# The inverse roots of 14 norms taken on two columns per token and spread by products with the identity; the output written in four transfers

## The chip, the cores and the metric

One NeuronCore of a Trainium2 chip runs the whole program. Its engines work side by side and wait for each other on semaphores: TensorE (PE: matmuls, and PEld: the loads of their stationary operand), VectorE (DVE), ScalarE (ACT), GpSimd (POOL) and SyncE (SP, which here issues the transfers of the weights and of the output). The metric is the device time of one execution in microseconds; a time is the median of several runs.

## What is computed

The reference runs two stacks of transformer-like blocks over 256 tokens with 1024 features (`x`), the first beside a second sequence of 256 context tokens (`ctx`). Each block opens its two halves with an RMS norm whose result is scaled and shifted by vectors made from a condition:

```python
def rms_norm(x, g):
    xf = x.astype(jnp.float32)
    y = xf * lax.rsqrt(jnp.mean(xf * xf, axis=-1, keepdims=True) + RMS_EPS)
    return (y * g.astype(jnp.float32)).astype(x.dtype)

def modulate(h, shift, scale):
    return h * (1 + scale) + shift
...
h = modulate(rms_norm(x, norm_g[i, 0]), sh1, sc1)
```

In the first stack the output of a mixer or of an MLP is normed as well before it is added to `x`. The second stack adds it without a norm, and ends in `rms_norm_2(x, final_g)`, which is the output. All told the kernel takes 17 such norms: one at the start, and 16 for which the line numbers below stand. What matters of them is one number for each token, the inverse root of the mean square over its 1024 features.

## The kernel before

Activations lie features first: a tile is [128 features, 256 tokens], and `KT` = 8 tiles make the 1024 features of a sequence. The sequences are called segments, `CTX` = 0 and `X` = 1. A sum over features is therefore a sum over partitions, and TensorE makes it: `sums_tensor` (L867) multiplies a 128x128 matrix of ones with the squares of tile k and adds the eight tiles up in PSUM. Since all 128 columns of the ones give the same sum, the result stands in every one of the 128 rows, and the root (`root_scalar`, L904, on ACT) and the reciprocal (`inverse_root_vector`, L911, on DVE) are taken on the whole [128, 256] tile `RS`. A float32 product is two records in the trace, so the eight products of one segment are 16 records. For six of the norms POOL adds the first six squares up beforehand, and TensorE has three products (6 records) instead of eight.

The places have names by what is normed: `y_x01`, `y_x02`, `y_x11`, `y_x12` are outputs of a mixer or an MLP, `n2_0`, `n1_1`, `n2_1`, `n1_2`, `n2_2`, `n1_3`, `n2_3` the residual stream, `final` the output. `y_x01`, `n2_0`, `y_x02` and `n1_1` exist for both segments.

At a place of the residual stream the order is: `x_squares_scalar` (ACT, L935) squares a tile, the sums follow tile by tile (L883), then the root (L907), the reciprocal (L914), `scaled_vector` (DVE, L943: one instruction per tile), then `high_scalar` (ACT, L974), which rounds the shifted tile, and `low_vector` (DVE, L988), which keeps what rounding left. The products that follow (`MLP0.columns` and others, L549) multiply high by the weights' high part, high by their low part, and low by high, eight tiles each, so a tile of output is 24 products. Where y is normed, `normed_residual_vector` (L993) multiplies pairs of tiles of y by the inverse root (L1003, four instructions) and adds them to x (L1008, eight instructions); the order on DVE is pair 0, pair 1, add 0, 1, pair 2, add 2, 3, pair 3, add 4 to 7. So a place of y is followed at once by a place of x: `y_x01` by `n2_0`, `y_x02` by `n1_1`, `y_x11` by `n2_1`, `y_x12` by `n1_2`. These are called pairs below.

Every engine works its instructions off in the order in which the program gives them. The blocks at the end of the program (L3818 to L4066) write that order out by hand, one list for each engine. Around `n2_0` DVE's list is: reciprocal and residual for X, the same for CTX, then for X and after it for CTX: reciprocal, `scaled_vector`, `low_vector`. `unread_products(pe, n, bank)` (L890) puts n float32 products of 512 columns into TensorE's list whose result nobody reads.

PSUM has eight banks. `take_bank` (L445) gives them out by a counter, and TensorE waits until the holder before has been marked "taken":

```python
b = pool[bank_state["next"] % len(pool)]
bank_state["next"] += 1
if bank_state["holder"][b] is not None:
    pe.wait_ge(*after("taken", *bank_state["holder"][b]))
```

The pool is banks 0 to 6 where nothing else is said; the sums have bank 6 for X and bank 5 for CTX, and a call with one fixed bank moves the counter too. In the kernel before, 112 calls precede the first tile of `mlp0_tensor`, 488 the first of `mlp_split_tensor` and 708 the first of `od_tensor`. `mlp0_tensor` (L1597) takes the banks of its first four tiles before its first product, then works out those four tiles for X, and after them for CTX. The weights go through a ring of four slots that SP fills when TensorE or DVE has released a block.

## Time and profile before

| | |
|---|---|
| time, median of 3 runs | 2351.47 us (2351.32 to 2355.02) |
| the profiled execution | 2352.81 us, its span 2350.9 us |
| mean granted clock of TensorE | 0.973 |
| busy in the span | PE 95%, PEld 79%, DVE 61%, ACT 41%, POOL 4% |
| reciprocals of the 16 norms (L914) | 16 of 1.75 us on DVE |
| unread products, sums, roots | L894, L883, L907 |
| transfer of the output | 1024 KB, 3.9 us from issue to landing |

Busy time says that an engine had work, not that the end depended on it. A PE that is busy counts loads and the drain of its pipeline too, and may stream few columns. The granted clock is a share of full speed: 1.00 is 2.4 GHz, 0.50 is 1.2 GHz. In a timeline a line is `start, duration, engine, source line, operation`, consecutive records of one kind are merged, and the brackets say how long the engine sat idle before it and who ended that.

### The profile page before, as it was taken

What the parts mean: (1) busy time and instruction counts of PE and PEld (TensorE: products, weight loads), DVE (VectorE), ACT (ScalarE), POOL (GpSimd) and SP (SyncE); (2) the same over time, 40 slices, a digit from 0 to 9 for tenths busy, and PEclk for the clock granted to TensorE, in tenths of its full rate; (3) what the DMA queues carried; (4) which work ended last, traced back from release to release, by engine and by line L of the source; (5) the groups of instructions that cost most, each with busy time, mean ns of one, the idle gap of its engine ahead of it and who ended that gap; (6) DMA issues with size and microseconds to landing.
All of it is one profiled execution on the core that took longest, in us unless ns stands there. A gap on an engine that the chain in (4) does not pass through costs nothing.

```text
span 2350.9 us, 48675 instructions
## 1 busy us (share of the span) xinstructions
PE 2242.8 (95%) x21596; PEld 1852.2 (79%) x21596; DVE 1427.9 (61%) x2467; ACT 971.5 (41%) x1716; POOL 85.4 (4%) x83
## 2 busy tenths in 40 slices
PE   8999999999999999999999999998999999899997
PEld 5864478888867789999998899895677879677786
DVE  3273536867657366887763653465475876656576
ACT  2244333332313223433322563344355655545565
POOL 1000000000010000000000001020000002000000
PEclk9999999999999989999999999998999999999999
DMA  8335237656522100000003446444355853204484
GB/s 355 108 111 213 89 128 302 252 214 233 215 99 104 40 1 4 4 4 4 13 4 129 142 176 239 197 180 179 126 219 210 337 218 126 72 1 179 177 339 181
DMA packets 47314, 348.13 MB, mean 148 GB/s; under 512 B 5264, under 2 KB 5280, under 8 KB 5760
## 3 DMA queue, kind: packets, MB, share of 16 engines
q1 hardware_dynamic: 45936, 334.52, 37.8%
q0 software_dynamic: 1168, 10.50, 1.1%
q8 instruction: 170, 2.79, 0.5%
q14 instruction: 40, 0.33, 0.0%
HBM read 343.95 MB, written 1.05 MB: 147 GB/s over the span
## 4 chain that ended last, share of the span: by engine, by line
PE 52%; DVE 8%; ACT 3%; issue 1%; DVEq 0%; ACTq 0%
PE banks L549 10%; PE banks L2245 6%; PE banks L2257 5%; PE banks L1037 4%; PE banks L3179 3%; PE banks L3180 3%; PE banks L3181 3%; PE banks L3210 2%; PE banks L3212 2%; PE banks L3211 2%; PE banks L2097 1%; PE banks L2304 1%; PE banks L561 1%; PE banks L2279 1%; PE banks L3228 1%
## 5 line engine op out<-in xcount | busy, mean ns | idle before, releaser
L527 DVE TENSOR_TENSOR mlp_w_low<-weight_slots,mlp_w_high 128x2048 fp32r<-128x2048 f32 x64 | 146.5, 2289 | 186.8 <-ACT mlp_w_high L518 186.8
L527 DVE TENSOR_TENSOR moe_w_low<-weight_slots,moe_w_high 128x2048 fp32r<-128x2048 f32 x96 | 217.9, 2289 | 61.6 <-ACT moe_w_high L518 60.8
L518 ACT ACTIVATE mlp_w_high<-weight_slots 128x2048 fp32r<-128x2048 f32 x64 | 122.4, 1912 | 177.8 <-PE banks L549 122.6
L518 ACT ACTIVATE moe_w_high<-weight_slots 128x2048 fp32r<-128x2048 f32 x96 | 181.7, 1914 | 23.6 <-PE banks L3212 19.8
L1037 PE MATMUL banks<-arena,weight_slots 128*128 128x256 f32 (+1 forms) x512 | 140.7, 436 | 3.0 <-DVE arena L2846 1.5
L3179 PE MATMUL banks<-moe_w_high,slots_x 128*128 128x512 f32 x320 | 130.6, 408 | 2.8 <-DVE moe_w_low L527 2.8
L1037 PEld LDWEIGHTS banks<-arena,weight_slots 128*128 128x128 f32 x512 | 97.8, 192 | 43.7 <-issue 33.6
L3180 PE MATMUL banks<-moe_w_low,slots_x 128*128 128x512 f32 x320 | 127.6, 399 | 0.0
L3181 PE MATMUL banks<-moe_w_high,slots_x 128*128 128x512 f32 x320 | 127.5, 398 | 0.0
L686 DVE SCALAR_TENSOR_TENSOR arena<-weight_slots,silu_c,arena 128x256 f32<-128x256 f32 x240 | 99.4, 483 | 0.0
L2245 PE MATMUL banks<-arena 64*64 64x64 f32 (+1 forms) x1600 | 81.9, 234 | 0.0
L2245 PEld LDWEIGHTS banks<-arena 64*64 64x64 f32 x1600 | 78.3, 139 | 0.5 <-issue 0.3
L1281 ACT ACTIVATE arena<-arena 128x256 f32<-128x256 f32 (+2 forms) x128 | 62.3, 489 | 38.8 <-DVE arena L1225 38.7
L864 POOL TENSOR_TENSOR arena<-arena 128x256 f32<-128x256 f32 (+1 forms) x30 | 36.5, 1216 | 1031.9 <-ACT arena L1683 407.8
L3179 PEld LDWEIGHTS banks<-moe_w_high,slots_x 128*128 128x128 f32 x320 | 60.7, 190 | 15.8 <-DVE moe_w_low L527 3.2
L3181 PEld LDWEIGHTS banks<-moe_w_high,slots_x 128*128 128x128 f32 x320 | 60.7, 190 | 14.7
L549 PE MATMUL banks<-quarter_high,mlp_w_high 128*128 128x512 f32 x256 | 67.4, 400 | 3.5 <-ACT quarter_high L1674 3.4
L3180 PEld LDWEIGHTS banks<-moe_w_low,slots_x 128*128 128x128 f32 x320 | 60.9, 190 | 12.4
L614 PE MATMUL banks<-weight_slots,arena 128*32 128x256 f32 x896 | 65.1, 414 | 4.5 <-DMA weight_slots<-weights 4.5
L549 PE MATMUL banks<-both_high,mlp_w_high 128*128 128x512 f32 (+1 forms) x288 | 68.3, 375 | 0.9 <-ACT both_high L974 0.8
L2257 PE MATMUL banks<-weight_slots 64*64 64x32 f32 x2048 | 66.6, 221 | 1.2 <-DVE weight_slots L2719 1.2
L2504 ACT ACTIVATE weight_slots<-banks 128x256 f32<-128x256 f32 x64 | 23.0, 382 | 107.7 <-DVE weight_slots L2709 107.2
(454 smaller groups left out, 5211.1 us busy)
## 6 DMA issues: line engine op xcount, KB each, us to landing
weight_slots<-weights SPq DMA_DIRECT2D x318, 1024.0 KB, 4.9
arena<-small POOLq DMA_DIRECT2D x1, 2560.0 KB, 9.0
arena<-x_t POOLq DMA_DIRECT2D x1, 2048.0 KB, 12.8
arena<-bias POOLq DMA_DIRECT2D x1, 2048.0 KB, 11.4
constants<-consts POOLq DMA_DIRECT2D x1, 1395.0 KB, 17.9
out_t<-arena SPq DMA_DIRECT2D x1, 1024.0 KB, 3.9
parameters<-params POOLq DMA_DIRECT2D x1, 763.0 KB, 21.8
arena<-pool_inv POOLq DMA_DIRECT2D x1, 512.0 KB, 14.6
```

Source lines behind the costliest of these rows:

```text
L518: nc.scalar.activation(self.pair(j)[0], slot(j, 0, SLOT), ACT.Copy).then_inc(*act.step("high", j))
L527: nc.vector.tensor_tensor(self.pair(j)[1], slot(j, 0, SLOT), self.pair(j)[0], ALU.subtract).then_inc(*v.step("used", j))
L549: ins = nc.tensor.matmul(out, self.pair(j)[part][:, at:at + P], x(k), start=start and n == 0 and k == 0, stop=stop and n == 2 and k == til ...
L614: ins = nc.tensor.matmul(psum(7, n % 2 * 256, 256, slice(32 * g, 32 * g + 32)), Z[:, 22 + 32 * k - n // 2 * 2:][:, 0:32], slot(j, k, 256), ...
L686: nc.vector.scalar_tensor_tensor(a_, w, c, a_, ALU.mult, ALU.add).then_inc(*v.step())
L1037: ins = nc.tensor.matmul(psum(b, 0, w), slot(j, k, 256, i * P, P), moving(k), start=(k == 0), stop=(k == KT - 1))
L1281: nc.scalar.activation(S[:, u % N, c:c + w], S[:, u % N, c:c + w], ACT.Exp, bias=M[:, u % N, 3 + j:4 + j], accum_out=M[:, u % N, 6 + j:7 + ...
L2245: ins = nc.tensor.matmul(psum(b, n * width, width, r), lhs, rhs, start=(i == 0), stop=(i == len(ts) - 1))
L2257: ins = nc.tensor.matmul(psum(b, p * 32, 32, half(h)), lhs(p, half(h)), rhs(p, half(h)), start=opens, stop=True, skip_group_check=True)
L3179: nc.tensor.matmul(psum(b), x_hi, wh, start=(k == 0), stop=False)
L3180: nc.tensor.matmul(psum(b), x_hi, wl, start=False, stop=False)
L3181: ins = nc.tensor.matmul(psum(b), x_lo, wh, start=False, stop=(k == KT - 1))
```

## The change

- At 14 places (all but `y_x02` and `n1_1` for CTX) the sums are turned around: the squares are the stationary operand, 128 tokens at a time, and one column of ones moves. The sums then stand one token to a row, in two columns. Root and reciprocal work on [128, 2].
- `spread_root_tensor` brings them back to [128, 256]: two products of a column of `RS`, broadcast to 128x128, with the identity. The result stands in the upper half of the bank of the sums, and `scaled_vector`, `normed_residual_vector` and `final_vector` read it there. The bank is "taken" only when the last of them that needs it has run: the eighth instruction of L943, or the fourth of L1003.
- TensorE's list: the unread products that stood before and after the sums are split, two ahead of each spread at most places, the rest behind; none ahead of the spreads of `n2_0`, where both segments' sums come first, then both spreads, then `mlp0_tensor`.
- DVE's list: both reciprocals of `y_x01` come ahead of both residuals. The order at `n2_0` stays.
- The output goes out in four transfers of two tiles each, each after its second tile.

```diff
+        def by_token(key, seg):
+            return seg == X or key in ("y_x01", "n2_0")
+        def root_at(key, seg):
+            return {("y_x01", X): 2, ("y_x02", X): SEQ}.get((key, seg), 0)
+        def spread_root_tensor(pe, key, seg):
+            b = take_bank(pe, ("spread", key, seg), [SUMS_BANK[seg]])
+            pe.wait_ge(*after("inverse_root", key, seg))
+            for t in range(2):
+                ins = nc.tensor.matmul(psum(b, SEQ + t * P, P), RS[:, seg, t:t + 1].to_broadcast([P, P]), cn("ident"),
+                                       start=True, stop=True)
+            ins.then_inc(*pe.step("rms", key, seg))
+        def inverse_roots(key, seg):
+            return psum(bank_of(("spread", key, seg)), SEQ, SEQ) if by_token(key, seg) else RS[:, seg, :]
...
+                if by_token(key, seg):
+                    for t in range(2):
+                        ins = nc.tensor.matmul(psum(b, at + t, 1), x[:, t * P:(t + 1) * P], cn("ones", 0, 1),
+                                               start=opens and i == 0 and t == 0, stop=(k == KT - 1), skip_group_check=True)
...
+            w = 2 if by_token(key, seg) else SEQ
+            nc.scalar.activation(RS[:, seg, 0:w], psum(bank_of(("sums", key, seg)), root_at(key, seg), w), ACT.Sqrt,
...
+            if by_token(key, seg):
+                part = RS[:, seg, 0:2]
+                nc.vector.reciprocal(part, part).then_inc(*v.step("inverse_root", key, seg))
...
+            if by_token(key, seg):
+                v.mark("taken", "spread", key, seg)
...
+            r = inverse_roots("y_" + key, seg).unsqueeze(1).to_broadcast([P, 2, SEQ])
...
+                    if k == KT - 2 and by_token("y_" + key, seg):
+                        v.mark("taken", "spread", "y_" + key, seg)
...
         def moe_tensor(pe, l):
-            unread_products(pe, 4, 0)
+            unread_products(pe, 2, 0)
+            spread_root_tensor(pe, f"n2_{l + 2}", X)
+            unread_products(pe, 1, 0)
...
-            for k in range(KT):
+            for k in (1, 3, 5, 7):
                 sp.wait_ge(*after("final", k))
-            eng.dma_start(out_t, HT[:, X].rearrange("p a b -> p (a b)")).then_inc(*sp.step(by=16, sem="out_written"))
+                eng.dma_start(out_t[:, (k - 1) * SEQ:(k + 1) * SEQ], HT[:, X, k - 1:k + 1].rearrange("p a b -> p (a b)")).then_inc(
+                    *sp.step(by=16, sem="out_written"))
...
-            x_sums_tensor(pe, "n2_0", [X, CTX], 5)
+            unread_products(pe, 2, 0)
+            for seg in (X, CTX):
+                spread_root_tensor(pe, "y_x01", seg)
+            unread_products(pe, 3, 0)
+            x_sums_tensor(pe, "n2_0", [X])
+            x_sums_tensor(pe, "n2_0", [CTX])
+            for seg in (X, CTX):
+                spread_root_tensor(pe, "n2_0", seg)
             unread_products(pe, 1, 0)
             mlp0_tensor(pe)
...
-            x_sums_tensor(pe, "n1_2", ONE, 5)
-            unread_products(pe, 4, 0)
+            unread_products(pe, 2, 0)
+            spread_root_tensor(pe, "y_x12", X)
+            unread_products(pe, 3, 0)
+            x_sums_tensor(pe, "n1_2", ONE)
+            unread_products(pe, 2, 0)
+            spread_root_tensor(pe, "n1_2", X)
+            unread_products(pe, 1, 0)
             ev2_tensor(pe)
...
             x_sums_tensor(pe, "n1_3", ONE)
-            unread_products(pe, 4, 0)
+            unread_products(pe, 2, 0)
+            spread_root_tensor(pe, "n1_3", X)
+            unread_products(pe, 1, 0)
...
             x_sums_tensor(pe, "final", ONE)
+            spread_root_tensor(pe, "final", X)
...
             for seg in (X, CTX):
                 inverse_root_vector(v, "y_x01", seg)
+            for seg in (X, CTX):
                 normed_residual_vector(v, "x01", 0, 0, seg)
```

The pairs `y_x02`/`n1_1` and `y_x11`/`n2_1` are edited as `y_x12`/`n1_2` is; behind the spread of `n1_1` stand four unread products.

## Rows read from the trace of the kernel before

**Rows 1.** Page, part 1: busy us, share of the span and count.

```profile
PE 2242.8 (95%) x21596; PEld 1852.2 (79%) x21596; DVE 1427.9 (61%) x2467; ACT 971.5 (41%) x1716; POOL 85.4 (4%) x83
```

**Rows 2.** One line's instructions: duration ns min/median/max, first and last start.

```profile
L914 DVE RECIPROCAL arena<-arena x16: 1743/1753/1754, 269.2 to 2341.5; 128x256 f32<-128x256 f32 x16
L883 PE MATMUL banks<-arena,constants x164: 377/379/595, 265.9 to 2340.6; 128*128 128x256 f32 x152, 128*128 128x512 f32 x12
```

**Rows 3.** Timeline of the pair `y_x12`/`n1_2`, PE, ACT and DVE.

```profile
1509.03 1.46 PE L883 MATMUL banks<-arena,constants 128*128 128x256 f32 x6
1510.33 4.46 PE L894 MATMUL banks<-constants 128*128 128x512 f32 x10
1511.03 1.75 DVE L914 RECIPROCAL arena<-arena 128x256 f32<-128x256 f32 x1 [4.51 <-ACT arena L907]
1512.82 1.29 DVE L1003 TENSOR_TENSOR arena<-arena 128x512 f32<-128x512 f32 x2
...
1515.11 1.10 PE L883 MATMUL banks<-arena,constants 128*128 128x256 f32 x4 [0.33 <-ACT arena L935]
...
1516.22 0.68 DVE L1003 TENSOR_TENSOR arena<-arena 128x512 f32<-128x512 f32 x1
...
1519.84 0.47 ACT L907 ACTIVATE arena<-banks,constants 128x256 f32<-128x256 f32 x1 [0.89 <-PE banks L883]
...
1522.20 3.26 DVE L943 SCALAR_TENSOR_TENSOR arena<-arena,modulations 128x256 f32<-128x256 f32 x8
...
1528.90 1.10 PE L549 MATMUL banks<-h_high,ev_w_high 128*128 128x256 f32 x8
```

**Rows 4.** Timeline around `n2_0`: second residual, sums, scaling, first tile of mlp0.

```profile
278.43 1.29 DVE L1003 TENSOR_TENSOR arena<-arena 128x512 f32<-128x512 f32 x2
...
283.41 1.99 PE L883 MATMUL banks<-arena,constants 128*128 128x256 f32 x8 [0.27 <-ACT arena L935]
...
285.79 3.26 DVE L943 SCALAR_TENSOR_TENSOR arena<-arena,modulations 128x256 f32<-128x256 f32 x8
...
287.02 3.25 PE L549 MATMUL banks<-both_high,mlp_w_high 128*128 128x256 f32 x8 [0.76 <-ACT both_high L974]
288.96 3.25 DVE L988 SCALAR_TENSOR_TENSOR both_low<-arena,modulations,both_high 128x256 fp32r<-128x256 f32 x8
290.07 1.91 PE L549 MATMUL banks<-both_high,mlp_w_low 128*128 128x256 f32 x8
...
293.37 1.12 PE L549 MATMUL banks<-both_high,mlp_w_high 128*128 128x256 f32 x8
```

**Rows 5.** Timeline: 128x128 loads with four moving columns, in the expert stage.

```profile
1730.33 2.29 PE L3241 MATMUL banks<-arena,places 128*128 128x4 f32 x20
```

**Rows 6.** Stretches: length, PE and PEld busy, DVE, ACT, POOL, PEclk, DMA share, GB/s.

```profile
290.00:292.00 2.00, 2.00 (x11) 2.00 (x11) 2.00 (x6) 0.00 (x0) 0.00 (x0) 0.50 0.00 0
...
1730.10:1733.60 3.50, 3.50 (x27) 3.27 (x26) 3.50 (x2) 1.23 (x2) 0.00 (x0) 1.00 0.16 35
1733.60:1737.00 3.40, 3.40 (x11) 2.51 (x10) 0.90 (x3) 0.00 (x0) 0.00 (x0) 0.51 0.96 388
```

**Rows 7.** Timeline: the shortest instructions of ACT and PE, and DVE reading PSUM.

```profile
1706.27 0.35 PE L3135 MATMUL banks<-arena 128*128 128x4 f32 x2 [0.41 <-DVE arena L3298]
...
1706.92 0.20 ACT L779 ACTIVATE table_touch<-constants 128x1 f32<-128x1 f32 x1
...
2336.12 3.23 DVE L3421 SCALAR_TENSOR_TENSOR arena<-banks,modulations,arena 128x256 f32<-128x256 f32 x8 [0.84 <-PE banks L3228]
```

**Rows 8.** Timeline of the end of the span.

```profile
2341.00 0.47 ACT L907 ACTIVATE arena<-banks,constants 128x256 f32<-128x256 f32 x1 [1.21 <-PE banks L883]
...
2343.30 3.26 DVE L3810 SCALAR_TENSOR_TENSOR arena<-arena,parameters 128x256 f32<-128x256 f32 x8
```

**Rows 9.** Page, part 6: DMA issues, KB each, median us to landing.

```profile
out_t<-arena SPq DMA_DIRECT2D x1, 1024.0 KB, 3.9
...
arena<-small POOLq DMA_DIRECT2D x1, 146.5 KB, 2.4
```

More of the change, by code:

```diff
@@ L882, in sums_tensor @@
                 k_at = k
-            ins = nc.tensor.matmul(psum(SUMS_BANK[segs[-1]], 0, len(segs) * SEQ), cn("ones"), squares_of(key, segs, k_at),
-                                   start=opens, stop=(k == KT - 1))
+            squares = squares_of(key, segs, k_at)
+            for i, seg in enumerate(segs):
+                x = squares[:, i, :] if len(segs) == 2 else squares
+                at, b = root_at(key, seg), SUMS_BANK[segs[-1]]
+                if by_token(key, seg):
+                    for t in range(2):
+                        ins = nc.tensor.matmul(psum(b, at + t, 1), x[:, t * P:(t + 1) * P], cn("ones", 0, 1),
+                                               start=opens and i == 0 and t == 0, stop=(k == KT - 1), skip_group_check=True)
+                else:
+                    ins = nc.tensor.matmul(psum(b, at, SEQ), cn("ones"), x, start=opens and i == 0, stop=(k == KT - 1),
+                                           skip_group_check=True)
             if k == KT - 1:
@@ L894, in unread_products, with x_sums_tensor @@
                 nc.tensor.matmul(psum(bank), cn("ones"), CN[:, 0:512], start=True, stop=True)
-        def x_sums_tensor(pe, key, segs, unread=0):
+        def x_sums_tensor(pe, key, segs):
             pe.stage("norm")
-            if unread:
-                unread_products(pe, unread, 0)
             for seg in segs:
@@ L902, in x_sums_tensor, with root_scalar @@
                     sums_tensor(pe, key, [seg], k)
-        def root_scalar(act, key, seg, at=0):
+        def root_scalar(act, key, seg):
             act.wait_ge(*after("sums", key, seg))
-            nc.scalar.activation(RS[:, seg, :], psum(bank_of(("sums", key, seg)), at, SEQ), ACT.Sqrt,
+            w = 2 if by_token(key, seg) else SEQ
+            nc.scalar.activation(RS[:, seg, 0:w], psum(bank_of(("sums", key, seg)), root_at(key, seg), w), ACT.Sqrt,
                                  bias=cn("eps", 0, 1), scale=1.0 / D).then_inc(*act.step("root", key, seg))
@@ L991, in low_vector, with normed_residual_vector @@
                     v.mark("h_low", key, k)
-        def normed_residual_vector(v, key, m, half, seg, x=XT):
+        def normed_residual_vector(v, key, m, half, seg, x=XT, tiles=(0, KT)):
             v.stage("residual")
@@ L997, in normed_residual_vector @@
             v.wait_ge(*after("rms", "y_" + key, seg))
-            r = RS[:, seg, :].unsqueeze(1).to_broadcast([P, 2, SEQ])
+            r = inverse_roots("y_" + key, seg).unsqueeze(1).to_broadcast([P, 2, SEQ])
             made = {}
-            for k in range(0, KT + 2, 2):
-                if k < KT:
+            for k in range(tiles[0], tiles[1] + 2, 2):
+                if k < tiles[1]:
                     y = YT[:, seg, k:k + 2, :]
@@ L1004, in normed_residual_vector @@
                     made[k] = v.own
-                if k >= 2:
+                    if k == KT - 2 and by_token("y_" + key, seg):
+                        v.mark("taken", "spread", "y_" + key, seg)
+                if k > tiles[0]:
                     v.wait_ge(*made[k - 2])
@@ L3883, in _ @@
                            banks=range(6), then=y_sums(pe, "x11", ONE))
-            x_sums_tensor(pe, "n2_1", ONE, 5)
-            unread_products(pe, 4, 0)
-            mlp_split_tensor(pe)
-            x_sums_tensor(pe, "n1_2", ONE, 5)
-            unread_products(pe, 4, 0)
+            unread_products(pe, 2, 0)
+            spread_root_tensor(pe, "y_x11", X)
+            unread_products(pe, 3, 0)
+            x_sums_tensor(pe, "n2_1", ONE)
+            unread_products(pe, 2, 0)
+            spread_root_tensor(pe, "n2_1", X)
+            unread_products(pe, 1, 0)
+            mlp_split_tensor(pe)
+            unread_products(pe, 2, 0)
+            spread_root_tensor(pe, "y_x12", X)
+            unread_products(pe, 3, 0)
+            x_sums_tensor(pe, "n1_2", ONE)
+            unread_products(pe, 2, 0)
+            spread_root_tensor(pe, "n1_2", X)
+            unread_products(pe, 1, 0)
             ev2_tensor(pe)
@@ L3905, in _ @@
             x_sums_tensor(pe, "n1_3", ONE)
-            unread_products(pe, 4, 0)
+            unread_products(pe, 2, 0)
+            spread_root_tensor(pe, "n1_3", X)
+            unread_products(pe, 1, 0)
             od_tensor(pe)
@@ L3929, in _ @@
             y_out_scalar(act, "x01", BOTH, lambda g: MLP0.high(act, g // 3 - 1) if g in (4, 6) else None)
-            root_scalar(act, "y_x01", X, SEQ)
+            root_scalar(act, "y_x01", X)
             root_scalar(act, "y_x01", CTX)
@@ L3938, in _ @@
             mlp0_scalar(act)
-            root_scalar(act, "y_x02", X, SEQ)
+            root_scalar(act, "y_x02", X)
             root_scalar(act, "y_x02", CTX)
@@ L4009, in _ @@
                 inverse_root_vector(v, "y_x01", seg)
+            for seg in (X, CTX):
                 normed_residual_vector(v, "x01", 0, 0, seg)
+            v.stage("norm")
             for seg in (X, CTX):
```

13 lines of the change are left out of this document (8 added, 5 removed).

## The prediction

> **What bounds the kernel now.** I read the page first: PE is busy for 95% of the span [rows 1]. So what can be won lies in the places where PE waits or only passes time, and the norms are such places. Then I went through the timeline from place to place, because a norm is a serial chain. The reader is to see it once in [rows 3]. The last sum ends at 1510.49 (1509.03 + 1.46). The root starts at 1510.53, the reciprocal at 1511.03 and takes 1.75, and DVE's next instruction starts at 1512.82: 2.33 us from sums to D, as I call the start of DVE's work. Meanwhile PE runs unread products: ten records in 4.46, one record drained, so about 0.43 each, 0.86 a product. At the second place of the pair the sums end near 1519.80 and D is 1522.20, 2.40. Around `n2_0` DVE works without a gap, and PE's first real tile is paced by it: it starts at 287.02, and the second tile only at 293.37, though later 24 products take about 2.9 (eight records in 1.12, 0.12 each) [rows 4]. Last I asked for the granted clock, since the change replaces streams of 256 columns by single ones.
>
> **The chain at one place.** Removed: 1.75 - of the reciprocal [rows 2], and part of the root's 0.47. Added: a root on two columns, about 0.24 (a one-column activation takes 0.20), a reciprocal on two columns and a wait of PE on DVE. No row has that reciprocal; between 0.05 (two of 256 columns of 1.75, and a start) and 0.25 I take 0.16. For the spread, two products are four records: no row has this form. Loads of 128x128 with four moving columns follow each other every 0.107 ((2.29 - 0.25) / 19) [rows 5], and a pair of them is 0.35 long [rows 7], so 0.6 to 0.8 for four and the waits at both ends. Bare, that is 0.04 + 0.24 + 0.04 + 0.16 + 0.9 = 1.4 instead of 2.33: a gain of 0.9. DVE then reads PSUM, which costs nothing: eight instructions from PSUM take 3.23, from SBUF 3.26 [rows 7, 4].
> But at most places two unread products lie on PE ahead of the spread. They start with the last sum and take 1.72 (four records of 0.43), then 0.33 + 0.27 + 0.1 for the spread and its drain: D = end of sums + 2.3. That is the reciprocal's time again. The sums themselves keep their rate: four records each 0.107 are 0.43 a tile, and two records of 256 columns 0.216 each are the same (six in 1.46, the last 0.38 long [rows 3, 2]); only the drain is 0.12 shorter. So a place with two unread products gains 0.15, not 0.9.
>
> **Pairs: the bank is held.** In a pair the spread of y occupies bank 6, which the sums of x want. It is released by the fourth L1003, which ends 4.08 after D (1516.90 against 1512.82); before, the sums began 2.29 after D, behind the first square [rows 3]. From 4.2 on, 32 records take 31 x 0.107 + 0.25 = 3.57: sums end at D + 7.8. Before it was 1519.80 - 1512.82 = 7.0. Loss 0.8, for three pairs (`y_x02`, `y_x11`, `y_x12`).
>
> **The clock.** Twenty loads of 128x128 with four moving columns run from 1730.33 to 1732.6; PE is busy for 3.50 of 3.50 us and PEld for 3.27, and yet the stretch behind it has a granted clock of 0.51 (1.2 GHz) [rows 5, 6]. The sums after the change are this kind of instruction, 32 in a row for 3.5 us, and in a pair PE idles for nearly 2 us before them. I therefore expect the clock at its lower level when the sums of x end. The two unread products on the chain then take up to 3.4 instead of 1.72, and the spread 0.4 more. At the lower level eight records of 256 columns take 1.91 instead of 1.12 [rows 4], so 0.23 against 0.12 each; the ratio of two holds for the long ones. The price lies between 0 and 2.1 a place; I take 1.7, since the twenty loads are the nearest row and part of the time may fall outside.
> The Trainium skill, page "TensorE: Matmul & The Clock Gate", Part 1 ("What's actually happening"), says that the clock follows how busy PE has been recently. Taken as busy time that would keep the clock up through the sums, and the sum would be that of the first rival; rows 6 speak against it.
> So a pair costs -0.15 + 0.8 + 1.7 = +2.35, three of them +7.0. `n1_3` (sums of eight tiles, no pair) costs -0.15 and the clock's price in part, 1.0: +0.85. `n2_2` and `n2_3` have only three tiles of sums behind the projection: -0.15 each, -0.3.
>
> **`n2_0`: PE waits behind DVE.** DVE's list is residual CTX, then for X reciprocal, scaling, low part, and only then the reciprocal for CTX. PE's list has the spread for CTX ahead of all of mlp0. Both reciprocals of y move ahead, so the CTX residual starts about 1.9 earlier (278.43 to 276.5: its own reciprocal of 1.75 and what `y_x01` gains); its fourth L1003 ends at 280.6, and the CTX sums take 3.57 from there: 284.25. Only then come both spreads; D for X is about 285.4 instead of 285.79. Scaling and low part take 3.26 and 3.25 [rows 4]: 291.9, plus the small reciprocal and the spread for CTX: 293.3. And there is a second wait. Four spreads more have moved the bank counter from 112 to 116, so mlp0's first four tiles have banks 4, 5, 6 and 0 and not 0 to 3. Bank 5 holds the CTX roots until the CTX scaling ends, 3.26 later: 296.6. `mlp0_tensor` takes all four banks first. PE starts real work at 296.7 instead of 287.02. All inputs are there then, so tile 0 takes 2.9 instead of 6.35. PE has done next to nothing for ten microseconds, so the clock starts low (it was 0.50 at 290 to 292 after much less of a pause [rows 6]); the low stretch in [rows 6] is 3.4 long, and one or two of these cost half of themselves, 1.7 to 3.4; I take 2.1. Tile 0 ends at 301.7 instead of 293.37: +8.3, between 6.2 (clock back at once) and 9.6 (two low stretches). Behind it PE works without a gap and nothing absorbs this. The transfers of weights are released by PE itself, so they come later too: SP's queue is not moved past anything.
> The same counter puts the first tile of `mlp_split_tensor` (488 + 8 = 496, bank 6) and of `od_tensor` (708 + 12 = 720, bank 6) behind the eighth scaling, D + 3.3. In [rows 3] the second tile follows at 1528.90, D + 6.7, because the low parts end there; 16 products of 0.12 still fit in between. Cover gone, that is where the clock is low, it costs up to 2.2; I take 0.5 each, +1.0. `ev2_tensor` gets bank 1 and is free.
>
> **The end.** No unread products precede the last spread. Sums end 0.1 earlier, and the chain is 1.4 at full clock and 1.9 at low instead of 2.34 (2340.96 to 2343.30 [rows 8]): -0.6. The transfer of 1024 KB takes 3.9 us from issue to landing, one of 146.5 KB 2.4 [rows 9]. The last of four has 256 KB and the others are out before it. Between 0 and 2.4 gained, I take 2.1 for its duration: -1.8. Together -2.4.
>
> **Sum.** 8.3 + 7.0 + 0.85 + 1.0 - 0.3 - 2.4 = +14.5 us on the profiled execution's 2352.81. Its time is 1.3 above the median of the runs, so I forecast 2351.5 + 14.5 = 2366.0. Terms at their bounds give +5 to +20.
>
> **Rivals.** (1) The clock holds through the sums. For it: 128x128 loads keep PE busy, and the end's 0.51 came only after a mixed stretch. Then `n2_0` costs 6.2, the pairs 0.65 each, the rest -0.15 - 0.3 - 2.8: +4.9, 2356.4. This is what the skill's rule on busy time would give. Against it: in [rows 6] PE was busy all the time before the clock fell. (2) Slower still: low stretches also fall on tile 0 of the two MLPs behind held banks, and mlp0 restarts in two of them: +20, 2371.5. (3) The other side, faster. DVE is what sets the pace around `n2_0` [rows 4], and it loses four reciprocals. If PE's first tile did not depend on the CTX spread and its bank, it would start 2.0 earlier; with a held clock, the three pairs' y gains alone (-0.45), -0.45 elsewhere and -2.8 at the end the sum is -5.7: 2345.8. It decides from the point where the CTX reciprocal runs before the X low parts, and where the sums of x don't wait for bank 6; by the lists neither is so.
>
> **Chances.** Forecast: 0.67, its own range 2360 to 2370. Rival (1) 0.18, (2) 0.10, (3) 0.05. The range of 2356 to 2371 leaves out (3), about half of (2) and some of (1). A measurement can tell 0.2%, 4.7 us, from no change: faster is below 2346.8 and is (3) alone, 0.05; the same, up to 2356.2, is nearly half of (1) and small slips of others, 0.10; slower 0.85.
>
> **What would show it.** L914 on 128x2 near 0.16 us; D 2.3 after the sums where the clock is 1.00 and over 4 where it is 0.50; the sums of x in a pair starting 4.1 after D; L549 of mlp0 starting near 297, right after the CTX scaling, with DVE's small reciprocal for CTX near 292; the granted clock at 0.50 in the unread products behind the sums; the last output transfer landing about 2 us after its issue. Wrong would I be most if PE's first L549 started before 290 or if the clock stayed at 1.00 through the single-column sums.

## The result

The changed kernel takes 2373.0 us in its profiled execution and between 2367.9 and 2377.9 us in four executions; a fifth took 2535.4 us at a mean granted clock of 0.827 and is left out. Against the kernel before, run beside it, the ratio is 1.0085, with an interval from 1.0072 to 1.0098: 20 us slower. The forecast was 2366.0, so 14.5 slower, with a range up to 2371. The direction held, the size did not.

From the page of the kernel after, its head, part 1 (which answers to [rows 1]) and the clock of part 2:

```profile
span 2371.2 us, 49098 instructions
PE 2255.3 (95%) x21804; PEld 1878.6 (79%) x21804; DVE 1404.8 (59%) x2467; ACT 967.6 (41%) x1716; POOL 84.2 (4%) x83
PEclk9999899999999998999999899999999999999999
```

DVE has lost 23 us of work, and PE is busy for 12.5 us more. The mean granted clock of the span fell from 0.973 to 0.962.

To see where the 20.3 us between the two spans arise I matched ACT's instructions one to one and took the difference of their starts. The middle columns are the start of the same instruction in both kernels, the fourth is its delay, the fifth what the stretch since the last line added, and the last what the forecast gave it.

| behind | before | after | delay | added | forecast |
|---|---|---|---|---|---|
| `n2_0`, mlp0 under way | 306.27 | 319.05 | 12.8 | +12.8 | +8.3 |
| pair `y_x02`/`n1_1` | 715.86 | 734.29 | 18.4 | +5.6 | +2.35 |
| first `wk` tiles | 751.31 | 763.22 | 11.9 | -6.5 | 0 |
| rest of `wkv` | 1271.72 | 1286.44 | 14.7 | +2.8 | 0 |
| pair `y_x11`/`n2_1`, first tile of the MLP | 1315.69 | 1336.48 | 20.8 | +6.1 | +2.85 |
| pair `y_x12`/`n1_2` | 1522.78 | 1546.12 | 23.3 | +2.5 | +2.35 |
| attention and router, `n2_2` | 1737.33 | 1756.61 | 19.3 | -4.0 | -0.15 |
| first experts, `n1_3`, od | 1992.54 | 2015.25 | 22.7 | +3.4 | +1.35 |
| attention, `n2_3`, second experts, the end | span | span | 20.3 | -2.4 | -2.55 |

### The profile after, place by place

`n2_0`. The timeline, chosen PE and DVE rows around it; its part from the scaling on answers to [rows 4].

```profile
265.33 2.73 PE L910 MATMUL banks<-constants,arena 128*128 128x1 f32 x24
267.92 3.55 PE L924 MATMUL banks<-constants 128*128 128x512 f32 x4
268.39 0.32 DVE L945 RECIPROCAL arena<-arena 128x2 f32<-128x2 f32 x2 [3.82 <-ACT arena L936]
271.26 1.20 PE L880 MATMUL banks<-constants,arena 128*128 128x128 f32 x8
272.13 1.28 DVE L1038 TENSOR_TENSOR arena<-arena,banks 128x512 f32<-128x512 f32 x2 [3.42 <-PE banks L880]
...
282.05 6.96 PE L910 MATMUL banks<-constants,arena 128*128 128x1 f32 x32 [0.75 <-ACT arena L968]
290.11 3.22 DVE L976 SCALAR_TENSOR_TENSOR arena<-arena,modulations,banks 128x256 f32<-128x256 f32 x8 [6.70 <-PE banks L880]
293.25 3.25 DVE L1023 SCALAR_TENSOR_TENSOR both_low<-arena,modulations,both_high 128x256 fp32r<-128x256 f32 x8
296.41 0.15 DVE L945 RECIPROCAL arena<-arena 128x2 f32<-128x2 f32 x1
296.71 1.19 PE L880 MATMUL banks<-constants,arena 128*128 128x128 f32 x4 [6.65 <-DVE arena L945]
...
306.16 1.12 PE L549 MATMUL banks<-both_high,mlp_w_high 128*128 128x256 f32 x8
```

The mechanism is the forecast one. DVE's small reciprocal for CTX stands behind the scaling and the low part of X (290.11 and 293.25), PE waits 6.65 for it, and the second tile starts at 306.16 instead of 293.37. What is new is the row at 282.05: the 32 single-column records take 6.96 us, 0.21 from one to the next, not 0.107. The stretches say why (length, PE, PEld, DVE, ACT and POOL busy, granted clock, DMA share, GB/s; as [rows 6]):

```profile
264.00:268.00 4.00, 4.00 (x29) 3.24 (x27) 0.54 (x6) 1.09 (x2) 0.00 (x0) 1.00 0.28 90
268.00:270.00 2.00, 2.00 (x4) 0.88 (x4) 0.32 (x2) 0.41 (x2) 0.00 (x0) 0.54 1.02 414
278.00:284.00 6.00, 5.25 (x28) 5.20 (x27) 5.41 (x13) 2.89 (x10) 0.00 (x0) 0.53 0.00 0
284.00:288.00 4.00, 4.00 (x20) 4.00 (x21) 0.00 (x0) 0.04 (x1) 0.00 (x0) 0.50 0.00 0
292.00:296.00 4.00, 0.00 (x0) 0.00 (x0) 4.00 (x11) 1.98 (x5) 0.00 (x0) 0.50 0.00 0
```

In 284 to 288 PE and PEld are both busy for all of the 4.00 us and the clock is at 0.50, its lower level of 1.2 GHz: some 20 loads in 4 us. In 264 to 268 PE is just as busy, at 1.00. The clock had dropped a first time behind the 24 single-column records of `y_x01` at 265.33, so that DVE got its roots at 272.13, 4.1 after the sums ended at 268.06.

The pair `y_x11`/`n2_1`, same view with rows chosen, answering to [rows 3], which shows the next pair of the kernel before. Of the 32 records of the second sums the last 20 are shown:

```profile
1310.41 1.40 PE L910 MATMUL banks<-constants,arena 128*128 128x1 f32 x12
1312.14 0.17 DVE L945 RECIPROCAL arena<-arena 128x2 f32<-128x2 f32 x1 [2.94 <-ACT arena L936]
1314.12 1.28 DVE L1038 TENSOR_TENSOR arena<-arena,banks 128x512 f32<-128x512 f32 x2 [1.81 <-PE banks L880]
1319.72 4.41 PE L910 MATMUL banks<-constants,arena 128*128 128x1 f32 x20
1323.98 3.76 PE L924 MATMUL banks<-constants 128*128 128x512 f32 x4
1324.16 0.26 ACT L936 ACTIVATE arena<-banks,constants 128x2 f32<-128x2 f32 x1 [3.95 <-PE banks L910]
1324.45 0.17 DVE L945 RECIPROCAL arena<-arena 128x2 f32<-128x2 f32 x1 [4.70 <-ACT arena L936]
1327.54 1.06 PE L880 MATMUL banks<-constants,arena 128*128 128x128 f32 x4
1328.64 3.22 DVE L976 SCALAR_TENSOR_TENSOR arena<-arena,modulations,banks 128x256 f32<-128x256 f32 x8 [4.02 <-PE banks L880]
```

The stretches of its second half, columns as above:

```profile
1318.00:1322.00 4.00, 3.77 (x23) 3.77 (x24) 1.76 (x5) 1.64 (x5) 0.00 (x0) 0.68 0.00 0
1322.00:1326.00 4.00, 4.00 (x13) 2.97 (x14) 0.17 (x1) 0.26 (x1) 0.00 (x0) 0.50 0.00 0
```

The first place of the pair has the full clock: sums end at 1311.81, D is 1314.12, 2.31 later, as forecast (2.3). The second has it not: the last 20 records take 4.41, the reciprocal is done at 1324.62, and the spread starts only at 1327.54, because two unread products at half clock stand before it. D is 4.5 after the sums' end at 1324.13; forecast was "over 4 where it is 0.50". The other places follow the same pattern: all five sums of 12 records have D 2.31 behind them, and wherever 24 or 32 records stand in a row, the clock falls within them or in the microseconds behind.

The end, to be read beside [rows 8] and [rows 9]:

```profile
2359.80 3.63 PE L910 MATMUL banks<-constants,arena 128*128 128x1 f32 x32
2363.76 0.17 DVE L945 RECIPROCAL arena<-arena 128x2 f32<-128x2 f32 x1 [1.97 <-ACT arena L936]
...
2365.30 3.22 DVE L3849 SCALAR_TENSOR_TENSOR arena<-arena,parameters,banks 128x256 f32<-128x256 f32 x8 [1.38 <-PE banks L880]
```

and of the page's DMA issues (transfers, KB each, us to landing):

```profile
out_t<-arena SPq DMA_DIRECT2D x4, 256.0 KB, 2.3
```

Here the full clock lasts through the sums: the same 32 records take 3.63, and from their end at 2363.43 D is 1.87 later, since it falls only behind them.

### The profile page after: what moved, and what is told of

Same layout as the page of the kernel before. It is cut to its first block, busy times and chain, and to the rows that moved or that the text cites. A ratio compares the mean times of both kernels' runs of the same rounds, so it can differ in the third digit from the quotient of the medians.

```text
span 2371.2 us, 49098 instructions
## 1 busy us (share of the span) xinstructions
PE 2255.3 (95%) x21804; PEld 1878.6 (79%) x21804; DVE 1404.8 (59%) x2467; ACT 967.6 (41%) x1716; POOL 84.2 (4%) x83
## 3 DMA queue, kind: packets, MB, share of 16 engines
HBM read 343.95 MB, written 1.05 MB: 145 GB/s over the span
## 4 chain that ended last, share of the span: by engine, by line
PE 52%; DVE 8%; ACT 3%; issue 1%; DVEq 0%; ACTq 0%
PE banks L549 10%; PE banks L2282 6%; PE banks L2294 5%; PE banks L1074 4%; PE banks L3218 3%; PE banks L3220 3%; PE banks L3219 3%; PE banks L3249 2%; PE banks L3251 2%; PE banks L3250 2%; PE banks L2134 1%; PE banks L2341 1%; PE banks L561 1%; PE banks L2316 1%; PE banks L910 1%
## 5 line engine op out<-in xcount | busy, mean ns | idle before, releaser
L518 ACT ACTIVATE moe_w_high<-weight_slots 128x2048 fp32r<-128x2048 f32 x96 | 181.7, 1913 | 23.3 <-PE banks L3251 19.8
L2294 PE MATMUL banks<-weight_slots,arena 64*64 64x32 f32 x2048 | 65.8, 219 | 0.9 <-DVE arena L1534 0.8
## 6 DMA issues: line engine op xcount, KB each, us to landing
arena<-pool_inv POOLq DMA_DIRECT2D x1, 512.0 KB, 14.7
```

Source lines behind the costliest of these rows:

```text
L518: nc.scalar.activation(self.pair(j)[0], slot(j, 0, SLOT), ACT.Copy).then_inc(*act.step("high", j))
L2294: ins = nc.tensor.matmul(psum(b, p * 32, 32, half(h)), lhs(p, half(h)), rhs(p, half(h)), start=opens, stop=True, skip_group_check=True)
```

## The experiments

All kernels compute the whole output. Ratios are against the kernel before, run beside each, about 2352 us. The theory after the result: the clock falls in the single-column sums, and they take twice as long, as does what PE has to do behind them; at `n2_0` two waits are built in; and the counter of the banks gives back some 6 us at `wk`. The rivals were that the cost lies in the waits alone, that few columns have nothing to do with the clock, and that the small gain at `wk` is chance.

### The bank counter alone (e1)

The kernel before, with the counter six higher while the features are taken:

```diff
+            bank_state["next"] += 6
             features_tensor(pe)
+            bank_state["next"] -= 6
```

> The kernel before with one edit: the bank counter stands 6 higher while the features are computed, as the changed kernel's six spreads leave it, and is put back afterwards. Nothing else of the change. In the trace of before PE waits until 736.55 for ACT's last copy of the r projection (it frees bank 0), because the third tile of the k projection is given bank 0; 6 higher it is given bank 6, free long before. Theory (the offset between the two traces falls from 18.4 to 12.1 us there because of the counter): 5 to 6 us faster than before, about 2346.5. Rival (the offset falls because PE had slack behind the rounded mixes, whatever the banks): no change, within 1 us.

Measured: 2348.0 us, ratio 0.9982 (0.9972 to 0.9992), 4 us faster, between 2 and 7 by the interval, which the expected 5 to 6 fits. Matched instruction by instruction with the profile of before, the stretch of the table from 715.86 to 751.31 is 6.6 shorter in e1, and it was 6.5 shorter in the change. One row of the timeline of the kernel before:

```profile
736.55 3.83 PE L1855 MATMUL banks<-mix_k_high,wk_w_high 128*128 128x512 f32 x9 [4.83 <-ACT arena L1496]
```

and two of e1:

```profile
729.01 6.08 PE L1855 MATMUL banks<-mix_k_high,wk_w_high 128*128 128x512 f32 x24
733.87 0.37 ACT L1496 ACTIVATE arena<-banks 128x256 f32<-128x256 f32 x1
```

Before, one of the first `wk` tiles needs a bank that ACT's last copy of `r` holds, and PE stands for 4.83. In e1 PE starts 4.86 ahead of that copy. The changed kernel has the same (`wk` at 749.72, the copy at 754.47), because its spreads take banks from the same counter. That is a gain that has nothing to do with norms.

### Sums that move 128 columns (e2) and 32 columns (e9)

The changed kernel, but the sums by token multiply with 128 columns of ones, and the root reads one column of each 128:

```diff
-                        ins = nc.tensor.matmul(psum(b, at + t, 1), x[:, t * P:(t + 1) * P], cn("ones", 0, 1),
+                        ins = nc.tensor.matmul(psum(b, at + t * P, P), x[:, t * P:(t + 1) * P], cn("ones"),
```

> The changed kernel with one size changed: each product of the sums per token moves 128 columns of ones and not 1, and the root reads the first of each 128. Same number of instructions, loads and waits. Theory (single-column products let TensorE's clock fall, and then sums, unread products and spreads take twice as long): clock 1.00 through most sums, 32 records of sums in 3.6 us and not 4.4 to 7.0, 12 to 15 us faster than the changed kernel, about 2359 to 2361; mlp0 still starts late. Rival (the clock falls because PE waits, whatever the products stream): within 2 us of the changed kernel's 2373.

Measured: 2354.7 us, ratio 1.0008 (0.9998 to 1.0017): not to be told from the kernel before, and 18 us faster than the change. Timeline of e2:

```profile
280.90 3.84 PE L910 MATMUL banks<-constants,arena 128*128 128x128 f32 x32 [1.72 <-DVE arena L1041]
291.83 1.20 PE L880 MATMUL banks<-constants,arena 128*128 128x128 f32 x4 [6.65 <-DVE arena L948]
296.34 2.08 PE L549 MATMUL banks<-both_high,mlp_w_high 128*128 128x256 f32 x8 [1.61 <-DVE arena L979]
301.26 1.12 PE L549 MATMUL banks<-both_high,mlp_w_high 128*128 128x256 f32 x8
```

A stretch of it:

```profile
280.00:284.00 4.00, 3.10 (x27) 3.10 (x28) 2.50 (x7) 2.30 (x7) 0.00 (x0) 1.00 0.00 0
```

PE is busy for 3.10 of 4.00 us and the clock stays at 1.00. With the clock held in the sums, the forecast for `n2_0` comes true to half a microsecond: PE starts mlp0 at 296.34 (296.7 was forecast) and the second tile at 301.26 (301.7), 7.9 later than before. What the forecast lacked is the clock in the sums.

The profile of e2, matched as in the table of the result, tells what the clock cost at each place:

| | added in the change | added in e2 | forecast for the clock here |
|---|---|---|---|
| `n2_0` | +12.8 | +7.9 | 0 |
| pair `y_x02`/`n1_1` | +5.6 | +2.5 | 1.7 |
| pair `y_x11`/`n2_1`, first tile | +6.1 | +0.7 | 1.7 + 0.5 |
| pair `y_x12`/`n1_2` | +2.5 | +0.7 | 1.7 |
| first experts, `n1_3`, od | +3.4 | -0.3 | 1.0 + 0.5 |

The 0.5 are for the held banks, which were to cost something only at a low clock. The differences come to some 19 us, where 7.1 was forecast. (The 2.1 that the forecast had for a low clock in mlp0's first tile is not among them: e2 has the low clock there too, 0.50 from 292 to 300.) These are single executions, and long stretches that no edit touches differ by several us between them.

The 128 columns don't hold the clock everywhere. At `n1_3` of e2 it fell ahead of the sums, and 32 records took 4.74 and not 3.84:

```profile
1919.99 4.74 PE L910 MATMUL banks<-constants,arena 128*128 128x128 f32 x32
```

There the granted clock was 0.84 over 1916 to 1920 and 0.74 over 1920 to 1924, and 1.00 again over 1924 to 1928. At the other places of e2 the sums ran at 1.00.

The rival to this reading is that any larger product would do. So the same with 32 columns:

> As e2_wide_ones, but each product of the sums moves 32 columns of ones and not 128. [...] Rival (any product wider than a few columns holds the clock): about 2355 as with 128.

Its timeline and a stretch:

```profile
283.36 7.01 PE L910 MATMUL banks<-constants,arena 128*128 128x32 f32 x32 [0.75 <-ACT arena L971]
```

```profile
284.00:288.00 4.00, 4.00 (x20) 4.00 (x21) 0.00 (x0) 1.36 (x5) 0.00 (x0) 0.50 0.00 0
```

Measured: 2371.2 us, ratio 1.0076 (1.0059 to 1.0093), as slow as with one column, 7.01 for the 32 records. If 32 columns let the clock fall nearly as one does, 2366 to 2373 was expected, and this came true. So 32 columns behave here as one does, and 128 do not, with the same number of products in the same places. Where between 32 and 128 it changes was not measured.

### `n2_0` freed of both waits (e3), and both together (e5)

```diff
+            bank_state["next"] += 3
             mlp0_tensor(pe)
+            bank_state["next"] -= 3
...
             for seg in (X, CTX):
                 inverse_root_vector(v, "n2_0", seg)
+            for seg in (X, CTX):
                 scaled_vector(v, "n2_0", 0, 1, seg)
```

> The changed kernel with the two waits at n2_0 taken away by order and by place: DVE takes both reciprocals of n2_0 before the scaling of X, and the bank counter stands 3 higher during mlp0, so that its first four tiles have banks 0 to 3. Theory (these two waits hold PE's first tile): L549 starts about 1.2 us after DVE's first scaling and not 12 us after it, the first tile ends 8 us earlier, about 2365. Rival (the low clock alone makes n2_0 late): the start moves, but less than 3 us are gained, over 2370.

> The changed kernel with both cures at once: 128 columns of ones in the sums per token, and at n2_0 both reciprocals ahead of the scaling and mlp0's first four tiles on banks 0 to 3. Theory (two separate causes that add up): the wide ones alone gave 2354.7 and still start mlp0 at 296.3 in its span; without the waits the first tile ends 7 to 8 us earlier, so 2347. Rival (with the clock held, the late start was mostly hidden): over 2352.

e3 measured 2366.8 us, ratio 1.0060 (1.0043 to 1.0077), 6 to 7 us under the change. PE's first product starts 1.5 behind X's scaling, and the second tile at 296.61, 9.55 earlier than in the change:

```profile
289.95 3.22 DVE L976 SCALAR_TENSOR_TENSOR arena<-arena,modulations,banks 128x256 f32<-128x256 f32 x8 [0.60 <-PE banks L880]
291.48 2.79 PE L549 MATMUL banks<-both_high,mlp_w_high 128*128 128x256 f32 x8
296.61 1.12 PE L549 MATMUL banks<-both_high,mlp_w_high 128*128 128x256 f32 x8
```

e5, which is e2 and e3 together, measured 2344.9, ratio 0.9960 (0.9944 to 0.9976): 10 under e2. By the times, freeing `n2_0` is worth 6 to 7 with single columns and 10 with the clock held, and each of the two figures may be off by some 5. The traces are sharper: behind `n2_0` ACT is 9.5 earlier in e3 than in the change, and 9.7 earlier in e5 than in e2. So the two causes add up, and with both gone the change is faster than the kernel before. In e3's profiled execution, the slowest of its four (2371.3), only 1.7 of the 9.5 is left at the end; the rest went in later stretches that the edit does not touch, for the most part in attention.

### Own banks (e6) and one unread product ahead of the spread (e7)

e6 is e5 with the spreads of y in banks 3, 4 and 5 in place of 6, so that the sums of x find bank 6 free. e7 is e6 with one of two unread products moved behind each spread:

```diff
-            unread_products(pe, 2, 0)
+            unread_products(pe, 1, 0)
             spread_root_tensor(pe, "y_x02", X)
-            unread_products(pe, 3, 0)
+            unread_products(pe, 4, 0)
```

> As e5_wide_free, and the spread roots of y stand in banks of their own (3 and 4 for y_x01, 5 for y_x02, y_x11, y_x12), so that the sums of x don't wait for the fourth multiplication by the roots. Theory: in each pair the sums end 0.8 us earlier, and about 1 us at n2_0: 3.5 us less than e5_wide_free, 2343.5. Rival (the last square ends the sums anyway, since they catch up): no change against e5_wide_free.

> As e6_own_bank, with one unread product ahead of each spread and the other one behind it, at ten places. Theory (two unread products of 0.86 us are what the chain waits for between the sums and the spread, in place of the reciprocal): D 1.45 us after the sums and not 2.3, 8 us less than e6_own_bank, about 2335.5. Rival (the clock falls behind the shorter filling, or PE's work behind is not ready sooner): within 2 us of e6_own_bank.

e6: 2342.9, ratio 0.9959 (0.9944 to 0.9974), which can't be told from e5 by the times. The traces show it: from D of y to the end of the sums of x it is 7.95 us in e5 in each of the three pairs and 7.02 in e6, against 6.98 in the kernel before (1512.82 to 1519.80). The held bank costs 0.9 a pair; 0.8 was forecast. e7: 2334.5, ratio 0.9920 (0.9903 to 0.9936), 8.4 us under e6 for ten places. That it is so near ten times 0.86 is partly luck, as the two intervals allow 4 to 14. In the traces it holds at each place: from the end of the sums to D it is 2.20 or 2.27 in e6 and 1.34 to 1.43 in e7. The first place of the pair `y_x12`/`n1_2` in e6:

```profile
1509.48 1.50 PE L911 MATMUL banks<-constants,arena 128*128 128x128 f32 x12
1510.82 1.88 PE L925 MATMUL banks<-constants 128*128 128x512 f32 x4
1511.32 0.17 DVE L949 RECIPROCAL arena<-arena 128x2 f32<-128x2 f32 x1 [4.34 <-ACT arena L940]
1512.54 0.61 PE L881 MATMUL banks<-constants,arena 128*128 128x128 f32 x4
```

and in e7:

```profile
1497.28 1.50 PE L911 MATMUL banks<-constants,arena 128*128 128x128 f32 x12
1498.62 1.02 PE L925 MATMUL banks<-constants 128*128 128x512 f32 x2
1499.12 0.17 DVE L949 RECIPROCAL arena<-arena 128x2 f32<-128x2 f32 x1 [4.34 <-ACT arena L940]
1499.48 0.61 PE L881 MATMUL banks<-constants,arena 128*128 128x128 f32 x4
```

In e6 the spread waits 1.05 us after the reciprocal is done, for its own engine; in e7 0.19. The unread products ahead of the spread are on the chain, as forecast.

### The best version (e8), and two steps back from it (e10, e11)

In e8 the spread for X at `n2_0` stands behind the third of CTX's sums, its reciprocal between the halves of CTX's residual, and CTX's spread behind mlp0's first four tiles (one more unread product stands ahead of mlp0):

```diff
+            for k in range(3):
+                sums_tensor(pe, "n2_0", [CTX], k)
+            spread_root_tensor(pe, "n2_0", X)
+            for k in range(3, KT):
+                sums_tensor(pe, "n2_0", [CTX], k)
...
+            mlp0_tensor(pe, lambda: spread_root_tensor(pe, "n2_0", CTX))
```

> As e7_one_unread, and at n2_0 the spread for X stands in PE's list after the third sum of CTX, its reciprocal in DVE's list between the halves of the CTX residual, and the spread for CTX behind mlp0's four tiles of X. Theory (X need not wait for the sums of CTX): the scaling of X starts as soon as the CTX residual ends, about 2 to 3 us earlier than in e7_one_unread, about 2333. Rival (ACT's root for CTX ahead of the rounding of X keeps PE waiting): no change.

Measured: 2332.2 us, ratio 0.9914 (0.9897 to 0.9930): 20 us faster than the kernel before and some 40 than the change. From e7 it gained 2, less than the two intervals can tell apart. e10 is e8 with single columns in the sums; e11 is e8 with no unread product ahead of a spread:

> e8_split with one change taken back: the sums per token move a single column of ones again. Theory (the clock is a cause of its own, whatever the order of the work): the low clock is back behind the sums, 12 to 18 us slower than e8_split's 2332, 2345 to 2350. Rival (in the changed kernel the low clock cost so much only because of the waits that e8_split has not): less than 5 us slower, below 2337.

> e8_split with no unread product ahead of any spread, all of them behind it. Theory (one product of 0.86 us is about as long as root and reciprocal on two columns with their waits, 0.5 us, so only 0.3 us a place is left): 2 to 3 us faster than e8_split, 2329.5. Rival (PE's idle half microsecond lets the clock fall): slower than e8_split by more than 2 us.

e10: 2340.8, ratio 0.9948 (0.9931 to 0.9964), so 8.5 slower than e8. It falls between what theory (12 to 18) and rival (under 5) expected: the clock is a cause of its own also in the best order of the work, but costs less there than the 18 between e2 and the change. The profiles show two reasons, though their sizes can't be taken from them (the two executions are 15.9 apart, e10's the slowest of its four and e8's the fastest). Behind the sums one unread product runs at half clock and not two: at the second places of the pairs and at `n1_3` D comes 2.3 to 2.8 after the sums for 1.4 in e8, and in the change it was 3.9 to 4.5 for 2.2 to 2.3 in e2. And the clock fell later: the longest sums of a pair take 4.48 in e10 and 5.89 in the change. At `n2_0`, counted from the first sums of `y_x01`, the price is about the same, 5.4 and 5.7. What sets the moment of the drop is open.

e11: 2336.8, ratio 0.9928 (0.9911 to 0.9944), 4.5 slower than e8 where 2 to 3 faster were expected. The intervals of the two overlap, so that it is slower is likely but not certain; the expected gain isn't there. The traces say why. At the first place of the pair `y_x12`/`n1_2` D is 1.34 behind the sums in e8 and 1.30 in e11, and at the other places they differ by no more than 0.02, not by 0.3. One unread product costs the chain nothing, and what is left is what the forecast called bare (1.4 instead of 2.33).

The rival, that the clock falls without the unread product, isn't borne out either. In e11's profile the granted clock is 1.00 from the first sum to D at every place, and the means of the four executions are 0.974 to 0.979 against 0.974 to 0.977 in e8. In the profiled executions, 7.7 apart, 3.0 of it arises in `wkv`, where no norm stands (519.5 us at a granted clock of 0.96 in e8, 522.5 at 0.95 in e11). Another part shows in the attention of the second stack, again far from the norms: the same 64 products in e8

```profile
1996.75 3.75 PE L3727 MATMUL banks<-arena 64*128 64x15 f32 x64
```

and in e11

```profile
2002.78 5.21 PE L3726 MATMUL banks<-arena 64*128 64x15 f32 x64
```

take 1.46 more in e11, where the granted clock is 0.85 over 2002 to 2006 and 0.50 behind that, while in e8 it is 1.00 over 1994 to 2002. PE's last work ahead of them is the same in both, down to its durations. Why the clock fell in one and not in the other, and whether the place of the unread products has a part in it, is open.

### The four transfers alone (e4)

```diff
-            for k in range(KT):
+            for k in (1, 3, 5, 7):
                 sp.wait_ge(*after("final", k))
-            eng.dma_start(out_t, HT[:, X].rearrange("p a b -> p (a b)")).then_inc(*sp.step(by=16, sem="out_written"))
+                eng.dma_start(out_t[:, (k - 1) * SEQ:(k + 1) * SEQ], HT[:, X, k - 1:k + 1].rearrange("p a b -> p (a b)")).then_inc(
+                    *sp.step(by=16, sem="out_written"))
```

> The kernel before with the output in four transfers of 256 KB as the changed kernel has it, and nothing else of the change. In the changed kernel's page a transfer takes 2.3 us from issue to landing, the single one of before 3.9. Theory: 1.6 us faster than before, about 2351. Rival (the four share a queue and the last lands no earlier): no change.

Measured: 2350.9, ratio 0.9996 (0.9987 to 1.0006), which can't be told from no change. In the profiled execution it shows: the last root starts 0.14 us earlier than before, and the span is 2349.1 against 2350.9, 1.8 shorter. The landing of the last transfer is 2.3 after its issue, where the single one took 3.9.

## Why the prediction held in direction and missed in size

- **The small reciprocal.** Taken at 0.16; the page has 14 of 128x2 at 0.17 (0.15 at the shortest). Right, as is that DVE reads its roots from PSUM for nothing: eight scalings take 3.22.
- **"A place with two unread products gains 0.15".** About right where the clock is full: 2.31 from sums to D against 2.33 before, 2.3 forecast, and six records of sums in 1.46 have become twelve in 1.40, so 0.1 gained.
- **"The sums themselves keep their rate".** This is the step that failed, and with it the term for the clock, 1.7 a place and nothing at `n2_0`. It holds at full clock (32 records in 3.63; 3.57 was forecast) and not at half, where they take 6.96. The text beside it expected the half clock "when the sums of x end", so it priced only the unread products and the spread behind them. But the drop comes inside the sums at `n2_0`, `n1_1` and `n2_1`, and the sums double too. Together the clock cost some 19 us and not 7.1. I had seen loads of 128x128 with four moving columns follow each other every 0.107 ahead of the drop [rows 5, 6], and took this for a rate that the clock does not touch. The trace of before has the row that tells otherwise, and I did not look for it:

```profile
2029.93 1.37 PE L3694 MATMUL banks<-constants,arena 128*128 128x128 f32 x8
```

  These eight products with a 128x128 load each start at a granted clock of 0.50 and end at 1.00; the first ones start 0.21 apart, the last ones 0.11.
- **`n2_0`.** Forecast +8.3, measured +12.8. Both waits are there, and with the clock held they cost what was worked out (e2: +7.9, starts within 0.5). The rest is 1.5 that the sums start later (282.05 against 280.6), since `y_x01` already pays for the clock, and 3.4 in the sums themselves: D for X at 290.11 instead of 285.4.
- **The pairs.** Forecast 2.35 each and 0.5 for the held bank behind one; measured 5.6, 6.1 and 2.5. The mechanism is right and the size is again that of the sums at half clock: in `n2_1` 20 records take 4.41 rather than 2.3, the unread products and spread 2.2 more. `n1_2` shows how much it depends on where the drop falls: its sums run at full clock but for the last 0.2 us, and D is 4.06 behind them. `n1_3` with what follows: +3.4 against 1.35, though its sums too run at full clock. The loss from bank 6 was put at 0.8 and is 0.9. With the clock held two of the three pairs cost 0.7, where the first rival had 0.65.
- **The held banks of `mlp_split` and `od`.** Their first tiles start with the end of the eighth scaling (1331.91 and 1943.84), as worked out. From D to the second tile it is 7.6 and 7.7 us, before 6.7 at both: 0.9 and 1.0 for the 0.5 forecast. In e2 it is 6.7 at both again, so the cost is that of the low clock, as forecast. The sum's upper end of +20 leaves these two at 0.5, though the text beside them allows 2.2 each; with that it would have been +23.
- **"Nothing absorbs this".** Wrong. At the first `wk` tiles 6.5 us came back, because the counter also moved a tile off a bank that was late. I followed the counter to the places where I feared a held bank and not to all places where PE waits for one; e1 shows that the gain exists without any norm.
- **The end.** Forecast -2.4, measured -2.4 with the expert stages, about -2.2 at the end itself. Right, in both its parts: the chain is 0.5 shorter (0.6 forecast), the landing 1.6 (1.8).
- **The rivals.** That the clock holds (the first) is refuted by the rows at 284 to 288. It was the case that followed from the Trainium skill, page "TensorE: Matmul & The Clock Gate", Part 1 ("What's actually happening"), if busy is read as busy time in a trace: this trace disagrees, with PE and PEld both at 4.00 of 4.00 us and the clock at 0.50. The third rival named conditions for a gain: the CTX reciprocal early, bank 6 not waited for and the clock held. e5 has the first and the last and gives 2344.9, e6 has all three and gives 2342.9, for its 2345.8. That they agree so well is partly chance, since both also have the gain at `wk` and the rival did not.

Taken together: 14.5, with 4.5 more at `n2_0`, 6.7 in the pairs, 2.1 at `n1_3`, 0.15 less gained behind it, 6.5 given back and -1.0 of the open part below, is the 20.3 of the spans to within rounding. The forecast erred by two misses of opposite sign, some 12 too little for the clock and 6.5 not seen at `wk`; that it came within 6 of the spans is owed to their cancelling. Without its terms for the clock in and behind the sums it says +7.4, with the 6.5 of `wk` +0.9, and the span of e2 is 2.1 longer than that of before.

What stays open: the delay also moves by +2.8 through `wkv`, where the change touches nothing, and by -4.0 through attention and router, where it touches only `n2_2`. In the second the granted clock was 0.94 in the profile of before and 0.98 in that of the change, 214.6 and 210.5 us long. In `wkv`, 520.4 and 523.2 long, it is 0.95 in both; among the profiles of the other kernels, which don't touch it either, this stretch is between 519.5 and 526.8 long. Why the low stretches fall there in one execution and not in another was not traced. e6 scatters more from execution to execution (2334.9 to 2351.5) than the kernel before (2347.6 to 2357.6), e7 and e8 less (within 1.8 and 3.2 us).

## What to carry to other kernels

Fewer moving columns didn't make these TensorE products cheaper: each comes with a 128x128 load, and at full clock they are 0.11 to 0.12 us apart with 1, 32 and 128 columns. But with few columns the clock fell, and all that followed paid: compare with a version that moves 128 columns before giving up the idea. When an engine's result is spread by TensorE, look at what stands between on its own list: a second filler product there cost 0.86 a place, one cost next to nothing, and taking that one away gained nothing. And if a rotating counter hands out banks, one more taker shifts every later holder: list all places where PE waits for a bank, those that may gain as well.

## What the runs showed of the hardware

- Records of 128x128 fp32 loads with one moving column follow each other every 0.11 at full clock (32 in 3.63, the last 0.25 long, in the change) and every 0.21 at half clock (32 in 6.96). With 128 columns at full clock it is 0.11 to 0.12 (32 in 3.74 to 3.84 in e2).
- The granted clock was 0.50 over 284 to 288 in the change and in e9, whose sums move 1 and 32 columns, with PE and PEld busy without a gap; over 280 to 284 of e2, with 128 columns, it was 1.00, with PE busy for only 3.10 of 4.00 us. Over 264 to 268 of the change PE was busy for 4.00 of 4.00 us too, and the clock 1.00. So busy time in the trace doesn't tell what the clock will do.
- 128 columns were no guarantee: at `n1_3` of e2 the clock was 0.74 over 1920 to 1924, in the sums.
- A reciprocal of 128x256 takes 1.75 us on DVE, one of 128x2 0.17. Eight scalings of 128x256 take 3.22 with the roots in PSUM and 3.26 with them in SBUF.
- The output's transfer of 256 KB lands 2.3 us after its issue, that of 1024 KB after 3.9.
